# Hybrid encoder layer on 8 cores: a pool of five PSUM banks, adaLN as dot products on VectorE, the relative bias without its constant part, and the value bias at evacuation

## What is computed

```python
mod = (silu(c) @ w_ada + b_ada).reshape(bsz, 9, 1024)     # adaLN
def sandwich(x, y_fn, g_pre, g_post, shift, scale, gate, weight):
    h = rms_norm(x, g_pre) * (1 + scale) + shift
    return x + weight * gate * rms_norm(y_fn(h), g_post)
# FFN: (silu(h @ w_gate) * (h @ w_up)) @ w_down, width 2816
# mixer: proj = h @ w_in + b_in; split into qa, ka, va, qb, kb, vb
# A: 8 query heads, 2 key/value heads, own chunk + 2 previous chunks of 64, ALiBi, sinks
# B: 8 heads, own chunk + 8 previous chunks, no sink, bias
rel_idx = clip(t - s, -128, 128) + 128
bias_b = rel_bias_b[:, rel_idx]
# each group is RMS-normalised, both are concatenated, then @ w_out + b_out
```

## Time and profile before

| | us |
|---|---|
| runs of this kernel | 1365.14, 1462.91, 1364.27 (median 1365.14) |
| the profiled execution's own time | 1369.62 |
| its span on the slowest core (core 7) | 1367.7 |
| spans of the eight cores | 1358.3 to 1367.7 |
| busy in the span, core 7: PE / DVE / ACT / POOL | 1285.5 / 457.3 / 447.7 / 188.1 |

### The profile page before, as it was taken

One profiled execution on the slowest core, in us unless ns is written; L12 is line 12 of the kernel. 1 busy time (PEld: TensorE's weight loads), 2 busy tenths in 40 slices (PEclk: granted clock), 3 DMA queues, 4 the chain that ended last, 5 costly groups with the idle time before them and its releaser, 6 DMA issues.

```text
span 1367.7 us, 21754 instructions; the slowest of 8 cores (1358.3 to 1367.7 us)
## 1 busy us (share of the span) xinstructions
PE 1285.5 (94%) x7941; PEld 611.2 (45%) x7941; DVE 457.3 (33%) x835; ACT 447.7 (33%) x902; POOL 188.1 (14%) x394
## 2 busy tenths in 40 slices
PE   2799999999989999999999999999998799999997
PEld 1344444554444444444444444444444344444443
DVE  2131122452454454222442122243143445522122
ACT  2241111342656552212341111233465655221110
POOL 3011101120121112101220000111011111200000
PEclk9999999999999999999999999999999999999999
DMA  9998977658243339993558756203542034899111
GB/s 174 173 201 144 169 130 125 113 88 158 47 85 73 69 69 163 169 156 122 170 144 156 126 101 113 38 0 65 91 84 41 2 63 92 146 162 159 43 47 61
DMA packets 32095, 148.24 MB, mean 108 GB/s; under 512 B 3274, under 2 KB 8567, under 8 KB 20344
## 3 DMA queue, kind: packets, MB, share of 16 engines
q0 software_dynamic: 26128, 129.64, 54.1%
q1 hardware_dynamic: 5864, 17.22, 3.5%
HBM read 258.36 MB, written 8.40 MB: 195 GB/s over the span
## 4 chain that ended last, share of the span: by engine, by line
PE 87%; DMA 4%; ACT 3%; DVE 2%; issue 2%; POOL 0%; DVEq 0%; ACTq 0%; POOLq 0%
PE psall L676 21%; PE psall L635 17%; PE psall L638 17%; PE psall L787 10%; PE psall L711 6%; PE psall L981 4%; DMA RING<-w_gu 3%; PE psall L878 3%; PE psall L725 2%; PE psall L916 2%; PE psall L888 1%; PE psall L666 1%; DMA R<-w_ada 1%; PE psall L524 1%; ACT R L894 1%
## 5 line engine op out<-in xcount | busy, mean ns | idle before, releaser
L676 PE MATMUL psall<-R 128*128 128x512 bf16 x1320 | 288.7, 379 | 0.0
L635 PE MATMUL psall<-HT,RING 128*128 128x512 bf16 x928 | 221.5, 382 | 6.0 <-DMA RING<-w_gu 4.9
L645 DVE TENSOR_TENSOR R<-SG,psall 128x512 bf16<-128x512 f32 x136 | 93.4, 687 | 381.3 <-ACT SG L643 357.7
L638 PE MATMUL psall<-HT,RING 128*128 128x512 bf16 x928 | 220.5, 381 | 0.0
L643 ACT ACTIVATE SG<-psall 128x512 f32<-128x512 f32 x136 | 81.2, 597 | 375.9 <-PE psall L638 375.7
L676 PEld LDWEIGHTS psall<-R 128*128 128x128 bf16 x1320 | 128.4, 98 | 151.2
L787 PE MATMUL psall<-HT,RING 128*128 128x512 bf16 x640 | 151.1, 387 | 4.2 <-ACT HT L509 2.4
L635 PEld LDWEIGHTS psall<-HT,RING 128*128 128x128 bf16 x928 | 90.7, 98 | 115.9 <-issue 10.8
L638 PEld LDWEIGHTS psall<-HT,RING 128*128 128x128 bf16 x928 | 91.2, 98 | 110.7 <-issue 3.1
L894 ACT ACTIVATE R<-psall 128x512 bf16<-128x512 f32 x202 | 109.7, 597 | 66.9 <-PE psall L888 50.9
L711 PE MATMUL psall<-HT,RING 128*128 128x512 bf16 x416 | 95.2, 380 | 0.2 <-ACT HT L509 0.2
(11 more groups left out here) (131 smaller groups left out, 1062.8 us busy)
## 6 DMA issues: line engine op xcount, KB each, us to landing
RING<-w_gu POOLq DMA_DIRECT2D x53, 1024.0 KB, 9.8
R<-w_down POOLq DMA_DIRECT2D x44, 512.0 KB, 17.3
R<-w_ada POOLq DMA_DIRECT2D x10, 1024.0 KB, 20.5
RING<-w_in POOLq DMA_DIRECT2D x10, 1024.0 KB, 9.9
RING<-w_ada POOLq DMA_DIRECT2D x8, 1024.0 KB, 9.8
out<-X SPq DMA_DIRECT2D x16, 512.0 KB, 2.6
R<-w_gu POOLq DMA_DIRECT2D x5, 1024.0 KB, 54.0
X<-x POOLq DMA_DIRECT2D x8, 512.0 KB, 27.2
```

Source lines behind the costliest of these rows:

```text
L635: e.matmul(PS[bG][:], lhsT=rb[:, k, jj * 128:(jj + 1) * 128], rhs=HT[:, k, tb * 512:(tb + 1) * 512], start=(k == 0), stop=(k == 7))
L638: ins = e.matmul(PS[bU][:], lhsT=rb[:, k, 256 + jj * 128:256 + (jj + 1) * 128], rhs=HT[:, k, tb * 512:(tb + 1) * 512], start=(k == 0), sto ...
L645: S.op('dve', (lambda e, bU=bU, sgi=sgi, j=j, tb=tb: e.tensor_tensor(out=AT[:, tb, j, :], in0=SG[:, sgi, :], in1=PS[bU][:], op=ALU.mult)), ...
L676: ins = e.matmul(PS[bk][:], lhsT=AT[:, t // 4, j, (t % 4) * 128:(t % 4 + 1) * 128], rhs=WD[:, j, hh * 512:(hh + 1) * 512], start=(j == 0), ...
```

## The change

Four parts.

1. **Banks.** Scores, fillers, output projection and transposes share one pool of banks 0, 1, 5, 6 and 7, and each takes the banks that the model holds free first. A bank with a running output projection is on hold. At most two are.
2. **adaLN on VectorE.** The 14 later pieces are read transposed (`w_adat`) and multiplied with a copy of silu(c) on all partitions: four dot products of 1024 elements per piece on VectorE (`tensor_tensor_reduce`, bf16, in place). A piece is spread over two steps: in `gu_phase` over two neighbouring steps (15/16, 17/18, 19/20, 21/22, 24/25, 26/27), in `down_mix` half before the tile's post-norm and half after its residual, ahead of the scale step. The last piece's second half stands in `mixer`, after the value projection of tile 0. The slot is released after the fourth dot product. At the start a 512 KB broadcast of c on SP's queue and one ScalarE pass over it are new.
3. **Bias.** Tables of B hold the bias minus its clipped value, so key tiles -2, -3 and -4 need no table matmul (15 pairs in half 0, 24 in half 1). The invisible quarter of key tile -4 is cleared after the exponential by a VectorE memset (24 in all). Two tables of 1024 columns are made at the start of the mixer instead of four in `down_mix`; the second waits for a 512 KB load into the buffer of the first.
4. **Value bias.** It is added at the evacuation, by VectorE, both for A and B; the 32 bias matmuls are gone, and ScalarE's copy too.

```diff
 # ring and adaLN
         def ada(i, hh, slot=None):
-            add(("ada", i, hh), full(wada_d[2 * i + hh]), slot)
+            n = 2 * i + hh - 4
+            add(("ada", i, hh), lambda slot: (rbuf(slot).rearrange("p k c -> p (k c)"), wadat_d[n]), slot)
...
+        dma_sp(CB0, c_d.rearrange("a b -> (a b)").partition_broadcast(128), [("cb0",)], ch=("c", 9))
+        S.op('act', lambda e: e.activation(out=SCB, in_=CB0, func=AF.Silu), reads=[("cb0",)], writes=[("scb",)])
...
-    def ada_item(i, hh):
+    def ada_dot(i, hh, cc):
         idx = plans[0][("ada", i, hh)]
-        ada_mm(rbuf(ring_slot[idx]), ring_keys(idx), i, hh)
-        ring_release(idx)
+        w = rbuf(ring_slot[idx]).rearrange("p k c -> p (k c)")[:, cc * 1024:(cc + 1) * 1024]
+        c0 = i * 8 + hh * 4 + cc
+        S.op('dve', lambda e: e.tensor_tensor_reduce(
+            out=w, in0=w, in1=SCB, scale=1.0, scalar=0.0, op0=ALU.mult, op1=ALU.add, accum_out=ADOT[:, c0:c0 + 1]),
+            reads=ring_keys(idx) + [("scb",)], writes=ring_keys(idx) + [("adot", c0)])
+        if cc == 3:
...
+            ring_release(idx)
+    def ada_dots(i, hh, half):
+        for cc in (2 * half, 2 * half + 1):
+            ada_dot(i, hh, cc)
 # down_mix
         def before(t):
-            ada_item(5 + t // 2, t % 2)
...
-            if 3 <= t < 7:
-                table_op(t - 3)
+            ada_dots(5 + t // 2, t % 2, 0)
         def after(t):
             if t < TPH - 1:
-                front(X[:, t, :], [("X", t)], t % 2)
+                c3 = front_square(X[:, t, :], [("X", t)])
+            if hf == 0 and t < 7:
+                ada_dots(5 + t // 2, t % 2, 1)
+                if t == 1:
+                    gg_col(1, 1.0)
+            if t < TPH - 1:
+                front_scale(X[:, t, :], [("X", t)], t % 2, c3)
 # start of the mixer
             proj_V(("win", 3, 0), t, (1, 6, 7, 0)[t])
             if t == 0:
                 front_scale(X[:, 7, :], [("X", 7)], 1, f7)
+                if hf == 0:
+                    ada_dots(8, 1, 1)
+                    gg_col(2, 0.5)
...
+                if hf == 0 and n in (1, 6):
+                    table_op(n // 6)
 # values
-                return e.matmul(PS[bank][:], lhsT=ONES[:, :], rhs=BHL[:, 0:512], start=False, stop=True)
-            S.op('act', lambda e: e.copy(out=VB[:, t, :].rearrange("p (h e) -> p h e", e=65)[:, :, 0:64],
-                                         in_=PS[bank][:].rearrange("p (h d) -> p h d", d=64)),
-                 reads=[ps_key(bank)], writes=[("VB", t)], regions=("R2",))
+            S.op('dve', lambda e: e.tensor_tensor(out=VB[:, t, :].rearrange("p (h e) -> p h e", e=65)[:, :, 0:64],
+                                                  in0=PS[bank][:].rearrange("p (h d) -> p h d", d=64),
+                                                  in1=BV[:, 0:512].rearrange("p (h d) -> p h d", d=64), op=ALU.add),
+                 reads=[ps_key(bank), ("bv",)], writes=[("VB", t)], regions=("R2",))
 # scores and banks
-        SBANKS = (0, 1, 5)
-        tyB = {0: 0, -1: 1, -2: 2, -3: 2, -4: 3}
+        pool = [0, 1, 5, 6, 7]
+        tyB = {0: 0, -1: 1}
+        def two_free():
+            return sorted([b for b in pool if b not in hold], key=lambda b: S.avail('pe', [], [ps_key(b)]))[:2]
...
-                for r in range(2):
+                plain = kind == "B" and ko not in tyB
+                for r in range(0 if plain else 2):
...
+            if kind == "B" and ko == -4:
+                for r in range(2):
+                    pi = (u + r) % NPT
+                    S.op('dve', (lambda e, pi=pi: e.memset(PT[pi].rearrange("p (h q) -> p h q", q=128)[0:64, :, 64:128], 0.0)),
+                         writes=[("pt", pi)], regions=(PTR[pi],), cost=0.2)
```

More of the change, by code:

```diff
@@ L517, in back @@
         src, skeys = XBUF[xb]
-        where = lambda k: (bank + 1, (k - 4) * 128) if split and k >= 4 else (bank, k * 128)
+        b0, b1 = (bank, bank + 1) if isinstance(bank, int) else bank
+        where = lambda k: (b1, (k - 4) * 128) if split and k >= 4 else (b0, k * 128)
         def fn(e):
@@ L739, in fn @@
                 for k in range(8):
[L740 to L747 removed]
+                    ins = e.matmul(PS[bank][:, 0:128], lhsT=HT[:, k, t * 128:(t + 1) * 128],
+                                   rhs=RING[:, slot, k, 128:256], start=(k == 0), stop=(k == 7))
+                return ins
+            S.op('pe', fn, reads=ring_keys(idx) + [("HT", t, k) for k in range(8)], writes=[ps_key(bank)], cost=0.5)
+            S.op('dve', lambda e: e.tensor_tensor(out=VA[:, t, :].rearrange("p (h e) -> p h e", e=65)[:, :, 0:64],
+                                                  in0=PS[bank][:, 0:128].rearrange("p (h d) -> p h d", d=64),
+                                                  in1=BV[:, 512:640].rearrange("p (h d) -> p h d", d=64), op=ALU.add),
+                 reads=[ps_key(bank), ("bv",)], writes=[("VA", t)], regions=("R2",), cost=0.25)
         S.op('pool', lambda e: e.memset(VA.rearrange("p t (h e) -> p t h e", e=65)[:, :, :, 64:65], 1.0),
@@ L769, in mixer @@
                     back(1, 7, 1, 4)
+                if hf == 0 and tag == ("win", 1) and g == 0:
+                    gg_row(2, 5)
+                if hf == 0 and n in (1, 6):
+                    table_op(n // 6)
                 proj_T(tag, g, dst3, g, b0 + g, name, 0, (2, 3, 1, 0)[n % 4])
@@ L856, in s_deps @@
             qk = [("QAT" if kind == "A" else "QBT", g, m // 4) for g in range(4)]
-            return kk[0 if kind == "A" else 1] + qk, [ps_key(SBANKS[(u + r) % 3]) for r in range(2)]
+            return kk[0 if kind == "A" else 1] + qk, [ps_key(b) for b in two_free()]
         def pv_deps(u):
@@ L872, in s_pair @@
             rd, banks = s_deps(u)
-            sb_ = [SBANKS[(u + r) % 3] for r in range(2)]
+            sb_ = [b[1] for b in banks]
             def fn(e):
-                for r in range(2):
+                plain = kind == "B" and ko not in tyB
+                for r in range(0 if plain else 2):
                     tab = EA[:, ko + 1, r * 4:(r + 1) * 4, :] if kind == "A" else EB[:, tyB[ko], r * 4:(r + 1) * 4, :]
@@ L888, in fn @@
                             ins = e.matmul(PS[sb_[r]][:, j * 128:(j + 1) * 128], lhsT=kb(j)[rows, :],
-                                           rhs=QBT[rows, j, tl], start=False, stop=(j == 3))
+                                           rhs=QBT[rows, j, tl], start=plain and j == 0, stop=(j == 3))
                 return ins
-            S.op('pe', fn, reads=rd + [("ea",), ("eb",), ("identb",)], writes=banks, regions=("R2",), cost=0.85)
+            S.op('pe', fn, reads=rd + [("ea",), ("eb",), ("identb",)], writes=banks, regions=("R2",), cost=0.36 if kind == "B" and ko not in tyB else 0.85)
             for r in range(2):
@@ L1004, in chain, with tb @@
             xh = [("xh", m % 2)]
-            bb = [ps_key(6), ps_key(7)]
-            ta = lambda: first_free([b for b in (6, 7) if b not in hold])
+            def tb(hh):
+                v["b", hh] = first_free()
+                tail_b(m, hh, v["b", hh])
             def sq(hh):
@@ L1040, in can_run @@
             need = steps[0][3]
-            if len(hold) == 2 if need is None else any(b in hold for b in need):
+            if len(hold) >= 2 and need:
                 return False
@@ L1060, in run_due @@
                     run_step(m)
-        def free_banks():
-            return cbanks if late[0] else [b for b in cbanks if b not in hold]
         def source(u):
```

170 lines of the change are left out of this document (93 added, 77 removed).

## The result

The changed kernel takes 1347.85 us (median of 4 runs, 1346.21 to 1349.37) against 1364.85: ratio 0.988, 95% interval 0.9866 to 0.9892. The forecast was 1331 with a range of 1312 to 1350. The direction is right and the time lies inside, but 17 us came where 34.4 were forecast.

A forecast was written before the change was run, and what follows sets the result against it. TensorE, busy 94% of the span, was taken as the bound. Terms -19.5, -4.4, -14.5, -12, +14 and +2 sum to -34.4 us: 1369.6 to 1335.2, less 4.5 gives 1331, range 1312 to 1350.

The forecast's parts named there:

- second table's load: Start of half 0's mixer: the second bias table waits for a 512 KB load, holding VectorE's evacuations; 1.5 us lost.
- pool: Attention stages: five shared banks let two pairs be in flight; half of 24.8 us idle, 12 saved, ends -4 and 20.
- bias tables of 39 pairs: Attention stages: 39 pairs lose two table matmuls each, at 0.50 us a pair; 19.5 us saved, ends 17 and 20.7.
- start +2: Before the first gate/up group: bound by transfers, and 512 KB more go in; 2 us lost, ends 0 and 3.
- whatever leaves TensorE's queue pays nearly in full: Whole kernel: TensorE's matmuls are busy 94% of the span, so work taken off it saves nearly its full time.
- The release step: Start of half 0's mixer: the last piece's slot is released 11.9 us after tile 7's matmuls; first query group waits 8.2.
- the first wait: Start of half 0's mixer: values of B wait 1.9 us for a w_in load needing adaLN piece 6's slot.
- the slow matmuls: Start of half 0's mixer: after the idle wait the granted clock falls; 2.5 us added.
- It fits, barely: Half 0's down tiles: VectorE's work with four dot products takes 9.4 us of the tile's 9.94.
- Slow dots: Rival, down tiles and adaLN steps of half 0: dot products near 2.5 us make the kernel 1385 us; chance 0.07.
- the pool without effect: Rival, attention stages: ScalarE's work stands in the way whatever the banks, so the pool brings nothing; 1343 us, chance 0.26.
- no load was on time: Rival, start of half 0's mixer: the late load causes no wait, by fast dots or short landing; 1317 us, chance 0.12.

The follow-up runs named there:

- e15: Changed kernel with old banks, adaLN back on TensorE and the plain pairs' table matmuls put back with zeros: 1378.6 us, 1.010 of before.
- e8: Changed kernel with adaLN back on TensorE and the 78 table matmuls of the plain pairs put back with zeros: 1346.7 us, 0.988 of before.
- e3: Changed kernel with adaLN back on TensorE matmuls, gate column and transpose still apart: 1338.3 us, 0.981 of before.
- e14: e8 with only a quarter of the second FFN's down weights loaded, its result not computed: 1337.1 us, 0.980 of before.
- e13: e3 with only a quarter of the second FFN's down weights loaded, its result not computed: 1325.7 us, 0.972 of before.
- e1: Changed kernel with the last adaLN piece's four dot products all ahead of tile 7's post-norm: 1337.9 us, 0.9805 of before.
- e5: Changed kernel with the broadcast of c started after the first four adaLN pieces, ScalarE's pass ten gate/up groups later: 1345.9 us, 0.987 of before.
- e2: Changed kernel with the first bias table made in tile 1 of half 0's first down phase: 1344.0 us, 0.985 of before.
- e10: e3 with the first bias table made in tile 2 of the first down phase: 1333.4 us, 0.977 of before.
- e4: Changed kernel with its bank part undone, scores on banks 0, 1, 5 and the rest on 6, 7: 1377.6 us, 1.009 of before.

## Why the prediction was wrong
The likeliest case had the right sign and named the large new wait; it was twice too hopeful. The kernels form a path from before to the changed one, and the forecast's terms can be put on it:

| step | forecast | measured | from |
|---|---|---|---|
| all parts but three: value bias -4.4, clears 0, gate column apart -3.2, second table's load +1.5 | -6.1 | +13.8 | before to e15 |
| pool | -12 | -30.2 | e15 to e8 |
| bias tables of 39 pairs | -19.5 | -9.8 | e8 to e3 |
| dot products for matmuls: -11.3, start +2, waits for w_in with slow matmuls +12.6 | +3.3 | +9.7 | e3 to changed |
| sum | -34.3 | -16.5 | |

(The forecast took 14 for 14.1, hence its -34.4.) The first two steps together were forecast at -18.1 and measured at -16.4. That is luck: each is off by 18 to 20 us, in opposite directions. What the total missed lies in the last two, 9.7 and 6.4 us.

*Bias tables: the step that failed most.* The size of the work was right, 19.2 us of busy time for 19.5. What failed is "whatever leaves TensorE's queue pays nearly in full". Half came back, since TensorE's idle time grew by 7.3 us (e14 to e13) in waits for VectorE above all. The forecast charged the idle of these stages to three score banks only, once, and took the tables' time on top. But this loss has nothing to do with the banks: it is the same with the old ones (9.0) as with the pool (9.8). "VectorE has room on the average" was read off shares of 33%; in the attention stages it is busy about half of the time, and TensorE waits for single operations of it. Which of VectorE's operations would have to go to get the other half was not tried.

*The adaLN part.* Against e3 the changed kernel differs in three stages (means of the eight cores):

| stage of half 0 | forecast | measured |
|---|---|---|
| start and gate/up | 2 - 4.9 = -2.9 | -0.5 |
| down | -6.5 | -5.5 |
| start of the mixer | +12.6 | +15.1 |

The release step was right in kind, by e1 and by the trace: the release was forecast 11.9 after tile 7's end (293.1, so 305.0) and came at 309.95, TensorE arrived later too, and the wait was 8.9 for 8.2. Mis-sized were the first wait, 4.6 for 1.9, and the slow matmuls, some 4 for 2.5. The forecast took the latter from two rows; at the first of them, 45.59, the granted clock reads 1.00 although the matmuls take twice their time, at the second 0.50.

The first wait traces to "It fits, barely". VectorE's work in a down tile was right, 9.5 us for 9.4. (A dot product is 1.22, the accumulator readout after it 0.08, and the next one starts 1.36 after it, 308.18 - 306.81; other operations start a little before the one ahead has ended.) What the term left out is that VectorE waits 0.8 us inside each tile, 0.17 between gate and residual and 0.62 before the scale step, for GpSimd's root:
```profile
279.10 0.90 POOL L517 TENSOR_SCALAR ST<-ST 128x1 f32<-128x1 f32 x1 [3.50 <-ACT SG L528]
280.83 0.75 DVE L535 TENSOR_SCALAR XH<-X,ST 128x1024 bf16<-128x1024 f32 x1 [0.62 <-POOL ST L519]
```
9.5 and 0.8 make the 10.29 of the tiles, against TensorE's 9.94, so each post-norm starts later than the one before, and so does each release. The root's first step took 0.90 and ended with the dot product beside it (278.70 to 279.93); before it took 0.22. An estimate from these rows: with 0.22 the wait of 0.62 would be gone, the tile 9.7, and TensorE the bound again. No run tried it. The Trainium skill (VectorE: DVE Perf Modes, "The perf-mode tier table") gives a plain tensor_tensor on bf16 in SBUF twice the rate. The dot product, bf16 with two sources, took 1.22 us and shows no doubling, as the row did not.

The start came 3.7 us later on core 7 and 3.2 as a mean of the cores, for 2 forecast. But e5, which takes those back, gains nothing clear of noise, and the six pieces moved off TensorE in the gate/up stage gained as little. Both terms were put where they do not set the time.

*The second table's load* was forecast at 1.5 and costs about 4 (e2) or 5.5 (e10).

*The pool.* The mechanism was right: waits for exponentials are gone with it (e8) and back without it (e4). The measured 30 lies outside its own end of 20. Half the idle of the trace before was taken as its worth, but e15, with old banks and the table matmuls, has 31 to 36 us of idle in the two attention stages, by core, where the kernel before has 25 to 27, and is itself 13.8 slower than that. A part's worth beside other new parts can't be read from the old trace's idle alone. Nor is 30 what the pool would give to the kernel before; no run has the pool alone.

*Left open.* Of the 13.8 us by which e15 is slower than the kernel before, the second table's load, the clears and the value bias account for about 5 (4 to 5.5, 2.6, -2.2); some 9 stay open, 12 with the gate column's forecast 3.2. By the stage starts of the two traces (means of the cores), e15 is 5.6 us longer in the start of half 0's mixer, 3.9 in its attention and 3.9 in half 1's mixer, and 3.6 shorter ahead of the mixer. In its attention stages TensorE waits for VectorE 16 to 18 us, by core, where it was 9 to 10. The planner orders these stages from modelled costs that the change altered; that the order is the cause was not tried.

*The rivals.* Slow dots did not come (1.22), the pool without effect is refuted by e4, and no load was on time.

## What to carry to other kernels
When work is moved to another engine, follow the buffer that it reads: its release moves with the work, and in a ring of few slots the next load is late by the full queue ahead of the new reader. Compare an engine's load per tile with the tile time including readouts and the waits for other engines inside the tile: here 9.5 us of work filled a tile of 9.94. Busy time taken off the busiest engine is not yet time gained, even where it is busy 95%: 19.2 us left TensorE and 10.8 came. One kernel per part, and one for each pair, tells which parts share a loss and which simply add.

## What the runs showed of the hardware
**Cores of a pair.** After the change one core of each pair is 10 to 15 us slower than its neighbour: 1331.7 and 1341.7, 1333.7 and 1344.2, 1328.9 and 1341.6, 1329.3 and 1344.7. Which one it is changes from run to run. At the end of half 0's mixer, core 7 then core 6:
```profile
510.00:545.00 35.00, 30.50 (x152) 13.92 (x150) 17.34 (x30) 10.29 (x24) 8.21 (x16) 0.95 0.90 152
```
```profile
510.00:533.00 23.00, 22.45 (x110) 10.02 (x107) 13.31 (x24) 7.17 (x16) 2.97 (x7) 1.00 1.03 186
```
The slower core gets 152 GB/s and idles 4.5 us, the faster 186 and 0.6. The kernel now comes up against the loads at this place, and the metric takes the slower core; with a quarter of the down weights (e13) all eight spans lie within some 6 us. Why the two cores of a pair get unequal shares was not tested.

**GpSimd beside dot products.** In half 0's down phase the first step of the root takes up to 1.29 us when a dot product runs on VectorE; in the kernel before it took 0.22 to 0.35 there:
```profile
283.93 1.25 POOL L517 TENSOR_SCALAR ST<-ST 128x1 f32<-128x1 f32 x1 [1.86 <-ACT SG L594]
```
It ends with the dot product that runs from 283.87 for 1.23. The same step at 299.48, with no dot product beside it, takes 0.22. The Trainium skill (SBUF — State Buffer, "Who interferes with whom") says that a VectorE instruction with two SBUF inputs contends with a GpSimd instruction that reads SBUF; the trace agrees, with 1.25 against 0.22 us; here it lengthens the tile, as told above.
